# Turns of the preceding pair moved from behind the scores into the middle of the next dense unit

## Time and profile before

| | |
|---|---|
| median of 3 runs | 1271.13 us (1270.64 to 1271.25) |
| the profiled execution | 1271.44 us |
| its span, first to last instruction | 1269.3 us |
| TensorE busy, matmuls | 1260.4 us (99%) |
| VectorE busy | 843.4 us (66%) |
| ScalarE busy | 678.6 us (53%) |
| GpSimd busy | 39.5 us (3%) |
| TensorE's mean granted clock | 0.999 |
| turns of probs in the trace | 160 transposes, from 307.7 to 1025.1 us |
| mean of DMA | 193 GB/s |

### The profile page before, as it was taken

The page is one execution under the profiler, slowest core; times in us unless marked ns, Lnnn a source line. Parts: engine busy times, 40 slices in busy tenths (PEclk is TensorE's granted clock), DMA queues, the critical chain, the costliest instruction groups (busy, mean ns, idle before and its releaser), DMA issues.

```text
span 1269.3 us, 17531 instructions
## 1 busy us (share of the span) xinstructions
PE 1260.4 (99%) x6763; PEld 1067.0 (84%) x6763; DVE 843.4 (66%) x1196; ACT 678.6 (53%) x920; POOL 39.5 (3%) x55
## 2 busy tenths in 40 slices
PE   9999999999999999999999999999999999999997
PEld 6888888888778888888888888888877788888886
DVE  6576667556778766566675665765567887655665
ACT  7454555445766355454554445554477653644444
POOL 0311100000000000000000000000000000000000
PEclk9999999999999999999999999999999999999999
DMA  7788755564644445555545555465556454555551
GB/s 272 240 288 250 251 206 199 199 221 164 228 142 172 169 168 196 198 183 183 179 184 199 198 186 182 161 211 195 191 198 209 125 194 171 185 196 198 198 192 40
DMA packets 59211, 245.05 MB, mean 193 GB/s; under 512 B 21344, under 2 KB 27616, under 8 KB 32408
## 3 DMA queue, kind: packets, MB, share of 16 engines
q1 hardware_dynamic: 58144, 242.54, 55.2%
q10 hardware_dynamic: 984, 1.80, 0.4%
q0 software_dynamic: 32, 0.02, 0.0%
HBM read 239.07 MB, written 5.27 MB: 192 GB/s over the span
## 4 chain that ended last, share of the span: by engine, by line
PE 97%; ACT 1%; DMA 1%; DVE 0%; issue 0%; POOL 0%; POOLq 0%; SPq 0%; ACTq 0%; DVEq 0%
PE bank L739 30%; PE bank L706 16%; PE bank L743 16%; PE bank L708 16%; PE bank L707 16%; PE bank L1042 2%; PE bank L1065 1%; PE bank L792 1%; PE bank L1056 1%; DMA params<-in_params 0%; DMA v<-in_lncount 0%; ACT whi L465 0%; PE bank L799 0%; ACT xT L590 0%; DVE wlo L1154 0%
## 5 line engine op out<-in xcount | busy, mean ns | idle before, releaser
L1154 DVE TENSOR_TENSOR wlo<-raw,whi 128x2048 fp32r<-128x2048 f32 x209 | 478.8, 2293 | 279.9 <-ACT whi L447 273.4
L447 ACT ACTIVATE whi<-raw 128x2048 fp32r<-128x2048 f32 x206 | 393.1, 1910 | 231.1 <-PE bank L743 140.8
L739 PE MATMUL bank<-xT,whi 128*128 128x512 f32 x1664 | 395.3, 390 | 0.0
L739 PEld LDWEIGHTS bank<-xT,whi 128*128 128x128 f32 x1664 | 308.7, 188 | 61.7
L743 PEld LDWEIGHTS bank<-xT,wlo 128*128 128x128 f32 x1664 | 207.2, 192 | 4.9 <-DVE wlo L1154 0.6
L743 PE MATMUL bank<-xT,wlo 128*128 128x256 f32 x1664 | 209.2, 283 | 0.1
L706 PE MATMUL bank<-whi,xT 128*128 128x512 f32 x432 | 171.6, 397 | 0.0
L708 PE MATMUL bank<-whi,xT 128*128 128x512 f32 x432 | 168.5, 390 | 0.0
L707 PE MATMUL bank<-wlo,xT 128*128 128x512 f32 x432 | 168.4, 390 | 0.0
L706 PE MATMUL bank<-whi,hTh 128*128 128x512 f32 x320 | 124.6, 389 | 0.1
L707 PE MATMUL bank<-wlo,hTh 128*128 128x512 f32 x320 | 124.5, 389 | 0.0
(11 more groups left out here) (160 smaller groups left out, 1058.7 us busy)
## 6 DMA issues: line engine op xcount, KB each, us to landing
raw<-in_stream SPq DMA_DIRECT2D x209, 1024.0 KB, 4.8
bias<-t_rows SPq DMA_DIRECT2D x24, 256.0 KB, 6.4
bias<-in_rpb SPq DMA_DIRECT2D x16, 256.0 KB, 7.8
masked<-bias SPq DMA_DIRECT2D x8, 512.0 KB, 6.9
bias<-masked SPq DMA_DIRECT2D x8, 512.0 KB, 4.6
raw<-in_stream SPq DMA_DIRECT2D x10, 256.0 KB, 7.0
x<-in_x SPq DMA_DIRECT2D x4, 256.0 KB, 5.5
raw<-in_stream ACTq DMA_DIRECT2D x2, 256.0 KB, 4.4
```

Of the source, the lines that this page charges most:

```text
L447: act.activation(whi[:, s, :], raw[:, s, :], ACT.Copy).then_inc(hi_ready, 1)
L739: return pe.matmul(dst[blk][:, :], whi[:, s, w], xT[:, 4 * a + k, :, :].rearrange("p a s -> p (a s)"), start=start, stop=stop)
L1154: dve.tensor_tensor(wlo[:, s, :], raw[:, s, :], whi[:, s, :].bitcast(F32), ALU.subtract).then_inc(unit_split, 1)
```

## The change

Only TensorE's order changes. `turn_probs(s)` is no longer issued at the end of step s + 1, behind the scores of pair s + 1, but in step s + 2 between the two halves of unit s + 2, through `mid`. This holds for all 12 pairs of both layers (steps 2 to 13). Nothing is changed on the other engines: their order and their waits stay. Unit 17, whose `mid` turns a quarter of the merged branches, keeps it.

```diff
                 for j, (kind, b, n, a) in enumerate(MIX):
                     pr = product_banks(j)
+                    turn_before = (lambda: turn_probs(j - 2)) if 2 <= j < PAIRS + 2 else None
                     before = products_read(j) if j and a == 0 else (None, None)
                     if kind == "gate":
-                        unit_rows(l, U_MIX + j, 0, xTh, xTl, 4 * a, pr, a == 0, a == 1, before=before)
+                        unit_rows(l, U_MIX + j, 0, xTh, xTl, 4 * a, pr, a == 0, a == 1, before=before, mid=turn_before)
                     else:
...
-                        turn_first = (lambda: turn_quarter(l, 2, 0)) if (b, n) == (BA, 1) else None
+                        turn_first = (lambda: turn_quarter(l, 2, 0)) if (b, n) == (BA, 1) else turn_before
                         unit_rows(l, U_MIX + j, 0, th, tl, k0, pr, True, True, before=before, mid=turn_first)
...
                     if 2 <= j < PAIRS + 2 and not ahead:
                         values(j - 2)
-                    if 1 <= j <= PAIRS:
-                        turn_probs(j - 1)
                     if j == PAIRS + 2:
```

## The result

The changed kernel takes 1280.22 us (median of 4 runs, 1279.3 to 1281.15) against 1270.89 us for the kernel before (4 runs, 1270.55 to 1271.25): a ratio of 1.0071, 95% interval 1.0057 to 1.0084. It is slower by 9.3 us; 1278.9 was forecast, +7.8. The profiled execution took 1281.15 us, its span 1279.1.

The account below looks back on a forecast made before the run. TensorE, busy for the whole stretch, was taken to bound the kernel. Order 2.5 us plus stalls 5.3 us for both layers gave +7.8, so 1278.9 us; the range for 8 in 10 was 1273.3 to 1282.5.

Parts of the forecast that it names:

- No gain possible: Stretch the change touches, 104.34 us in layer 0: TensorE is busy throughout, so reordering has no idle time to win back.
- The order: TensorE's changes between kinds of matmul: +0.12 us for each of pairs 0 to 8, 0.15 for pairs 9 to 11.
- exp at T + 4.50: ScalarE's exp of the next pair starts 4.50 us after unit start T, behind the copies of the later turns.
- The stalls: TensorE waits per layer: unit 4 0.43 us, units 8 and 9 0.05 each, unit 10 0.59, pair 8's values 1.55.
- Weights: Low parts of the weights split behind exp come later but before their units need them: hidden, no stall.
- The clock: An idle microsecond alone doesn't lower TensorE's granted clock, so the sum had nothing for it.
- Rival 3: Clock falls in the stall of pair 8's values, losing 1.2 us per layer: +2.3, 1281.2 us; chance 0.07.
- Rival 1: Waits stay covered, no stalls occur and only the order costs: +2.5 us, 1273.6; chance 0.12.
- Rival 2: Delay feeds itself: six other unit starts, 4 to 11, each wait 0.59 us: +7.1, 1286.0 us; chance 0.10.
- Rival 4: Faster: a first half behind scores costs the plain 2.73 us, turns get cheaper: -1.0 us, 1270.1; chance 0.05.

Follow-up runs that it names:

- e4: Changed kernel with TensorE's order kept, but the work it waits for issued at other places on ScalarE and VectorE, mostly earlier: 1273.14 us, ratio 1.0015.
- e7: Kernel before, with the turns moved for pairs 2, 3 and 4 alone: 1271.95 us, ratio 1.0002.
- e8: Kernel before, with scores issued ahead of values in the steps of branches C and B too, as branch A has them: 1271.64 us, ratio 0.9999.
- e2: Changed kernel plus 6 matmuls on data nobody reads, ahead of the wait of pair 8's values in both layers: 1278.54 us, ratio 1.0057.
- e1: The changed kernel run again with no edit, against the kernel before: 1280.46 us, ratio 1.0076.

## Why the prediction was right

The cause was right for 7.7 of the 9.3 us, and its close size is in part luck: a layer was forecast at 1.23 + 2.67 = 3.90 and came to 3.83 without a fall of the clock, because the order was put 0.4 too high and the waits 0.3 too low. A third term, the clock, was put at nothing and was not.

- **No gain possible**: right. TensorE had no idle time in the stretch, and every variant with moved turns is as slow or slower.
- **The order, +0.12 a pair, 1.23 a layer**: the mechanism was right, the size too large. e4 has some 0.83, e7 0.07 a pair. The mis-sized term is the first half behind scores, taken as 2.90 from unit 1, the one unit that stood there; in the middle of the stage it takes 2.86 (319.51 - 316.65), and only unit 2 takes 2.90. That is 0.04 to 0.05 for each of seven pairs, and pair 8 was put at 0.12 and costs nothing. The guess of 0.15 for pairs 9 to 11, for which no row stood, came to 0.20. The turns at 0.79 and the slow start behind them came out as read from the earlier trace rows.
- **exp at T + 4.50**: 4.46.
- **The stalls, 2.67 a layer**: some 3.0. Measured by how much later the next matmul starts than the 0.21 or 0.22 between scores and their successor: unit 4 0.55 (0.43 forecast; 325.70 shows 0.48 of it as idle), unit 8 0.08 and unit 9 0.17 (0.05 each), unit 10 0.69 (0.59), values of pair 8 1.66 (1.55). In part they are larger because TensorE comes to each wait earlier: a step lasts 8.50 us and not 8.54, and a first half behind a wait takes 2.81 to 2.85, not 2.90, so pair 8's values were due 7.00 behind the start of unit 10 and not 7.09. What they wait for was late by up to 0.08 more than forecast (unit 4's tanh). Part comes back in the quicker matmuls behind a wait, which is why these five add up to 3.15 and cost only 3.0.
- **Weights**: no unit waited for them, as worked out.
- **The clock**: wrong. I had "by the rows an idle microsecond alone doesn't lower the clock, and the sum has nothing for it", and named a clock below 1.00 in the stretch as what would prove me wrong. Layer 0 bears the sentence out and layer 1 refutes it. The step that failed is the reading of the earlier trace rows: how long the clock stays up behind the last matmul isn't one figure. TensorE's last matmul before that fall is in the window 1262 to 1263, over 4 us ahead of it; in layer 1 the fall came at about 1017.35, under 2 us behind the last of the scores and in the middle of new matmuls. The Trainium skill ("TensorE: Matmul & The Clock Gate", "HAM oscillation") says that an engine which stops between groups of matmuls can be given the low clock and begin the next group with it. The trace agrees in kind, in 2 stalls of 6, and not in the detail: the first matmuls behind the stall still ran at 1.00. The Trainium skill's example there is of waits longer than these, so it did not say that a stall of 1.6 us would do. Rival 3 had the place right and 1.2 us as its price; a fall cost 1.68 and 1.53. One fall is what lies between the forecast's +7.8 and what the two stretches of the first profile grew by: 2 x 3.83 = 7.66 without it, + 1.68 = 9.34 with it. The median is 9.33 over the kernel before, so a typical execution seems to have one fall, but only two executions of this kernel were profiled.
- **Rival 1** (waits covered, +2.5): refuted by the three waits in the trace; e4 shows what it would have given, +1.9. **Rival 2** (the delay feeds itself): ScalarE's copy waited for the turns, not they for it, and the other gate starts have no wait. **Rival 4** needed a first half of 2.73; it took 2.86.

## What to carry to other kernels

When TensorE never idles, an instruction moved within its queue can gain only what a cheaper change between kinds of matmul gives (0.04 us in e8); what it can lose is more, since it may release another engine later. Take the moved instruction's new end, add what is queued behind the waiting instruction on that engine, and hold the sum against TensorE's next need. Most such delays cost nothing (e7). The few that do may sit several steps away, on a bank or a tile that has nothing to do with what was moved (pair 8's values behind the split of branch B's o). If a stall can't be taken away, filling it with matmuls whose results nobody reads can pay (1.9 us in e2).

## What the runs showed of the hardware that was not expected

- Behind 1.6 us without a matmul the clock fell to 1.2 GHz in 2 of 6 profiled stalls. It still read 1.00 in the idle time and for 0.25 to 0.3 us of the new matmuls (up to 1017.3 in the changed kernel, 1016.6 in e1). Dense matmuls of 128x512 then lay 0.43 us apart, until it read 1.00 again at 1020.8. The stalls of 0.5 and 0.6 us were never followed by it.
- Six added matmuls in each of two stalls took 1.9 us off the median (1278.54 in e2, 1280.46 in e1).
- A unit directly behind scores, whose matmuls use 64 rows, loses 0.13 us in its first 12 matmuls (2.86 against 2.73); 12 behind transposes lose 0.11 (2.84). So eight transposes put into dense work cost their own 0.79 and one more slow start.
